# Hybrid decoder layer on one core: the mixer's output projection by seven block products for eight

## The reference, cut to what matters

```python
y = jax.nn.sigmoid(ga) * (att @ w_attn_br[l]) + jax.nn.sigmoid(gm) * (hm @ w_mlstm_br[l])
x = x + y @ w_out[l]          # (512 x 2048) @ (2048 x 2048): the product that is changed

hc = rms_norm(x, norm_cross[l])
cq = (hc @ w_cq[l]).reshape(b_, s_, CROSS_HEADS, CROSS_HEAD_DIM)
```

## Time and profile before

| what | before |
|---|---|
| median of 3 runs | 2763.83 us (2763.59 to 2771.11) |
| profiled execution | 2762.1 us, which is its span; nothing else is recorded of it |
| busy PE | 2716.5 us, 98% |
| busy DVE | 1951.8 us, 71% |
| busy ACT | 1205.3 us, 44% |
| granted TensorE clock | 0.995 of full speed in the mean |

### The profile page before, as it was taken

How to read it: one execution, slowest core, us unless ns; L and a number is a source line. 1 busy time by engine, 2 the same in 40 slices (tenths; PEclk the granted TensorE clock), 3 DMA queues, 4 the chain that set the end, 5 groups by cost and what they waited for, 6 DMA issues and landing times.

```text
span 2762.1 us, 35868 instructions
## 1 busy us (share of the span) xinstructions
PE 2716.5 (98%) x13169; PEld 2276.6 (82%) x13169; DVE 1951.8 (71%) x2483; ACT 1205.3 (44%) x1603; POOL 130.2 (5%) x194
## 2 busy tenths in 40 slices
PE   8999999999999999999998999999999999999998
PEld 7888888888788888888877888888888888888886
DVE  6674345454576556642346999999998999999998
ACT  6342234343433223322336566666665433333334
POOL 1000000000000000000000011111110000000000
PEclk9999999999999999999999999999999999999999
DMA  7454233324253222552214677777779955556533
GB/s 276 174 192 139 91 105 106 106 91 147 104 190 98 101 99 92 172 187 92 90 61 119 195 214 216 244 235 236 210 233 320 384 198 193 213 213 225 201 115 114
DMA packets 192136, 469.07 MB, mean 170 GB/s; under 512 B 11706, under 2 KB 32299, under 8 KB 180267
## 3 DMA queue, kind: packets, MB, share of 16 engines
q1 hardware_dynamic: 141512, 374.44, 38.6%
q10 hardware_dynamic: 33122, 76.61, 7.3%
q0 software_dynamic: 17408, 16.78, 4.2%
HBM read 366.08 MB, written 84.93 MB: 163 GB/s over the span
## 4 chain that ended last, share of the span: by engine, by line
PE 94%; DVE 2%; DMA 1%; ACT 1%; issue 1%; POOL 0%; ACTq 0%; DVEq 0%; POOLq 0%
PE acc L2281 13%; PE acc L2283 13%; PE acc L2282 13%; PE acc L2735 8%; PE aux L2735 6%; PE acc L2736 4%; PE acc L2765 4%; PE acc L2767 4%; PE acc L2769 4%; PE aux L2765 3%; PE aux L2769 3%; PE aux L2767 3%; PE aux L2736 3%; PE acc L2389 1%; PE acc L2393 1%; PE aux L2393 1%
## 5 line engine op out<-in xcount | busy, mean ns | idle before, releaser
L909 ACT ACTIVATE fhi<-flat 128x1024 fp32r<-128x1024 f32 x400 | 422.8, 1059 | 483.2 <-PE aux L2769 139.4
L1456 DVE TENSOR_TENSOR flo<-flat,fhi 128x1024 fp32r<-128x1024 f32 x400 | 487.2, 1220 | 70.6 <-ACT fhi L909 65.0
L1451 DVE TENSOR_TENSOR wlo<-raw,whi 128x2048 fp32r<-128x2048 f32 x112 | 256.7, 2292 | 310.6 <-ACT whi L895 309.7
L2281 PE MATMUL acc<-act_hi,whi 128*128 128x512 f32 x1024 | 406.8, 397 | 2.1 <-DVE vaug L1583 1.4
L2283 PE MATMUL acc<-act_hi,wlo 128*128 128x512 f32 x1024 | 400.0, 391 | 0.0
L2282 PE MATMUL acc<-act_lo,whi 128*128 128x512 f32 x1024 | 399.1, 390 | 0.0
L895 ACT ACTIVATE whi<-raw 128x2048 fp32r<-128x2048 f32 x112 | 213.8, 1909 | 298.8 <-PE acc L2283 282.6
L2281 PEld LDWEIGHTS acc<-act_hi,whi 128*128 128x128 f32 x1024 | 192.4, 188 | 43.7 <-issue 2.8
L2283 PEld LDWEIGHTS acc<-act_hi,wlo 128*128 128x128 f32 x1024 | 192.2, 188 | 41.1
L2282 PEld LDWEIGHTS acc<-act_lo,whi 128*128 128x128 f32 x1024 | 192.6, 188 | 37.4
L2735 PE MATMUL acc<-t,fhi 128*128 128x512 f32 x512 | 184.9, 401 | 12.4 <-issue 5.1
(11 more groups left out here) (393 smaller groups left out, 5675.0 us busy)
## 6 DMA issues: line engine op xcount, KB each, us to landing
raw<-in_w_in SPq DMA_DIRECT2D x64, 1024.0 KB, 5.1
flat<-in_w_up SPq DMA_DIRECT2D x64, 1024.0 KB, 7.7
flat<-in_w_down SPq DMA_DIRECT2D x64, 1024.0 KB, 5.1
hid_scratch<-staged ACTq DMA_DIRECT2D x112, 512.0 KB, 6.8
side_P<-hid_scratch SPq DMA_DIRECT2D x56, 1024.0 KB, 7.3
flat<-in_w_in SPq DMA_DIRECT2D x16, 1024.0 KB, 5.5
raw<-in_w_out SPq DMA_DIRECT2D x16, 1024.0 KB, 5.1
flat<-flat POOLq DMA_DIRECT2D x64, 256.0 KB, 3.8
```

Of the source, the lines that this page charges most:

```text
L909: nc.scalar.activation(tiles(fhi[ring(b, n)][:], down), unit_source(b, down, n), ACT.Copy).then_inc(unit_hi, 1)
L1451: nc.vector.tensor_tensor(wlo[n % 2][:], raw[n % 4][:], whi[n % 2][:].bitcast(F32), ALU.subtract).then_inc(lo_ready, 1)
L1456: nc.vector.tensor_tensor(tiles(flo[ring(b, n)][:], down), unit_source(b, down, n), tiles(fhi[ring(b, n)][:], down).bitcast(F32), ALU.subt ...
L2281: nc.tensor.matmul(dst, s_hi, v_hi, start=first, stop=False)
```

## The change

The output projection is made of four wide blocks of 14 units: for each half of the 2048 output columns, one block for y's tiles 0 to 7 and one for 8 to 15. The four sums of y's quarters that the products P6, P7, P5 and P3 need are made while y is made: `y_sums(i)` takes the two tiles 2i and 2i+1, ACT rounds them (`y_sums_hi`), DVE takes the rest (`y_sums_lo`), and ACT's queue stores both parts in DRAM (`store_y_sums`), from which SP loads them into `y_place` for each block. There is one staging pair, so `y_sums_hi(i)` waits for the store of sum i-1. The landing is `out_land`: two instructions on 128x512 for each product.

```diff
-N_WIDE = 4
+N_WIDE = 8
...
+Y_PLACE = {"P6": 0, "P7": 1, "P5": 2, "P3": 3}
+Y_SUMS = ("P6", "P7", "P5", "P3")
+X_SUMS, N_SUMS = 8, 16
...
+    out_blocks = [Wide_no(4 + i, G_CQ // 4 + 4 + i + 1, i == 0, out=i // 2) for i in range(4)]
+    out_blocks[3].set = 2
...
-        wide_blocks(w_out_v, G_OUT, 0, 1, 4)
...
+        sp.wait_ge(granule_used, G_CQ)
+        sp.wait_ge(y_sum_stored, Y_STORES + 32 * 7)
+        for name in Y_SUMS:
+            load_y_sum(out_blocks[0], name)
+        sp.wait_ge(y_sum_stored, Y_STORES + 32 * 8)
+        for j in range(2, 4):
+            residual(j)
+        for b, following in zip(out_blocks, out_blocks[1:]):
+            load_y_sum(following, "P6", b.units(6))
+            load_y_sum(following, "P7", b.units(8))
+            load_out(0, following, unit_lo, b.units(9))
+            load_out(1, following, unit_lo, b.units(10))
+            load_y_sum(following, "P5", b.units(10))
+            load_out(2, following, unit_lo, b.units(13))
+            load_out(3, following, unit_lo, b.units(14))
+            load_y_sum(following, "P3", b.units(UNITS))
...
+        def y_sums_hi(i):
+
+            act.wait_ge(sum_ready, X_SUMS + i + 1)
+            if i:
+                act.wait_ge(y_sum_stored, Y_STORES + 32 * i)
+            nc.scalar.activation(y_stage[0][:], y_sum_f[i % 2][:], ACT.Copy).then_inc(side_hi, 1)
+
+        def store_y_sums(i):
+
+            act.wait_ge(side_lo, X_SUMS + i + 1)
+            for part in range(2):
+                act.dma_start(y_sums_dram[i // 4, :, :, part, i % 4, :].rearrange("s p n -> p s n"),
+                              y_stage[part][:].bitcast(F32)).then_inc(y_sum_stored, 16)
+
         for j in range(4):
             for g in range(2):
-                split(G_MBR + 2 * j + g + 1)
+                if 2 * j + g < 7:
+                    split(G_MBR + 2 * j + g + 1)
+                if g == 0 and j:
+                    y_sums_hi(2 * j - 1)
+                elif j:
+                    store_y_sums(2 * j - 1)
+            if j == 3:
+                act.wait_ge(granule_used, G_CQ - 1)
+                unit_split_hi(out_blocks[0], 0, True)
+                unit_split_hi(out_blocks[0], 1, True)
...
+                if k % 4 == 2:
+                    y_sums_hi(2 * j)
+            store_y_sums(2 * j)
...
+        for q, b in enumerate(out_blocks):
+            for n in range(0 if q else 2, UNITS):
+                unit_split_hi(b, n, True)
+                if (q, n) == (0, 4):
+                    y_sums_hi(7)
+                if (q, n) == (0, 6):
+                    store_y_sums(7)
+                if q == 2 and n >= 6:
+                    out_squares(n - 6)
+                if q == 3 and n >= 7:
+                    query_input_hi(n - 7)
...
+        def y_sums(i):
+
+            f, first, second = y_sum_f[i % 2], ysum[0], ysum[1]
+            upper, lower = slice(0, 256), slice(256, 512)
+            step(nc.vector.tensor_tensor(f[:, 1, :], first[:, upper], first[:, lower], ALU.subtract))
+            step(nc.vector.tensor_tensor(f[:, 0, :], second[:, lower], f[:, 1, :], ALU.subtract))
+            step(nc.vector.tensor_tensor(f[:, 2, :], f[:, 0, :], first[:, upper], ALU.add))
+            nc.vector.tensor_tensor(f[:, 3, :], second[:, upper], f[:, 0, :], ALU.subtract).then_inc(sum_ready, 1)
...
+                if m == 1:
+                    y_sums(2 * j)
+                elif m == 2:
+                    y_sums_lo(2 * j)
+                elif m == 3 and j < 3:
+                    y_sums(2 * j + 1)
...
+        for n in (2, 3):
+            unit_split_lo(out_blocks[0], n, True)
+        for n in range(4):
+            weight_sum(out_blocks[0], DOWN_MIX_POS[n], True)
+        y_sums(7)
+        for q, b in enumerate(out_blocks):
+            for n in range(0 if q else 4, UNITS):
+                if q and n in (1, 3):
+                    out_land(out_blocks[q - 1], {1: "P4", 3: "P3"}[n])
+                if n in (5, 7, 9, 11, 13):
+                    out_land(b, PRODUCTS[(n - 5) // 2])
+                unit_split_lo(b, n, True)
+                if n in DOWN_MIX_POS:
+                    weight_sum(b, DOWN_MIX_POS[n], True)
+                if (q, n) == (0, 5):
+                    y_sums_lo(7)
+                if q == 3 and n >= 7:
+                    query_input_lo(n - 7)
+        out_land(out_blocks[3], "P4")
+        split(G_CQ)
+        query_input_lo(7)
+        out_land(out_blocks[3], "P3")
...
+            for n in range(UNITS):
+                wide_unit(b, n, banks_out, {name: (Y_PLACE[name], Y_LOADS // 16 + q + 1) for name in Y_SUMS}, (y_place, lambda p: y_place_loaded[p]), y_quarter)
+                if q == 3 and n >= 6:
+                    x1_tile(n - 6)()
```

More of the change, by code:

```diff
@@ L103, with __init__ @@
 SUM_LOADS = ((5, 5), (3, 0))
+Y_PLACE = {"P6": 0, "P7": 1, "P5": 2, "P3": 3}
+Y_SUMS = ("P6", "P7", "P5", "P3")
+X_SUMS, N_SUMS = 8, 16
 class Wide_no:
-    def __init__(self, i, loads):
-        self.turn, self.first, self.rows, self.opens, self.loaded = 0, i, i % 2, i % 2 == 0, 16 * (loads + i % 2 + 1)
+    def __init__(self, i, loads, opens=True, out=None):
+        self.turn, self.first, self.rows, self.opens = 0, i, i % 2, opens
+        self.loaded = 16 * loads
+        self.out, self.set = out, 1 - i % 2 if out is None else i % 2
     def units(self, i):
@@ L509, in mix_of @@
     def mix_of(b, u):
-        return wide_mix[b.first // 2][u] if isinstance(b, Wide_no) else mix[u]
+        if not isinstance(b, Wide_no):
+            return mix[u]
+        return wide_mix[b.first // 2][u] if b.out is None else out_mix[u]
     def unit_source(b, down, n):
@@ L523, in x_quarter, with y_quarter @@
         return part[:, 8 * row + 4 * rows:8 * row + 4 * rows + 4, 256 * half:256 * (half + 1)]
+    def y_quarter(part, rows, row, half):
+        return part[:, 8 * rows + row:8 * rows + 8:2, 256 * half:256 * (half + 1)]
     def sums_at(rows, name):
@@ L1204, in _, with squares @@
                 nc.scalar.activation(act_hi[:, k, :], ysum[k % 2][:], ACT.Copy).then_inc(y_hi, 1)
-        def squares(blk, m, j, done, before, turn=0):
-            act.wait_ge(bank_free[m], freed(blk, m, turn))
+                if k % 4 == 2:
+                    y_sums_hi(2 * j)
+            store_y_sums(2 * j)
+        def squares(ready, count, m, j, done, before):
+            act.wait_ge(ready, count)
             if before is not None:
@@ L1230, in _ @@
             query_input_hi(k)
+        for i in range(12, 16):
+            out_squares(i)
         split(G_CQ + 2)
@@ L2571, in _ @@
                     hooks={} if j else {(0, 1): [unit_transposes(NG - 1)]})
-        with pe.Fori(0, 3) as i:
-            product(B_OUT, G_OUT, 4, tokens(act_hi, act_lo), turn=i, n_per=4, inputs=waits(y_hi, y_lo))
         def residual_transposes(k, blk, full, hi, lo):
```

153 lines of the change are left out of this document (98 added, 55 removed).

## The result

The changed kernel takes 2800.4 us in the median of four runs (2795.8 to 2803.2) against 2763.8, 37 us slower; the ratio on record, made of all runs and not of the two medians, is 1.0123, interval 1.0103 to 1.0142. Forecast were 2783 and a range up to 2797: the direction came, the loss is twice the predicted one.

What follows compares the result with a forecast made beforehand. PE, busy 98% of the span, was taken to bound the kernel. Waits of 9.3 + 16.2 + 9.0 + 3.3 = 37.8 us, less 21.8 removed, plus 3 for the clock, gave 2763.8 + 19 = 2783 us, range 2770 to 2797.

Steps and rivals of the forecast that it cites:

- the landing L: mLSTM output: time from a sum store's second issue until it lands, taken as 7.5 us between ends of 4.9 and 12.7.
- share evenly: mLSTM output: stores and simultaneous loads split the transfers equally, so a second MB passes first, adding 2.6 us to 4.9.
- the 3 that stood for the clock: After waits: 3 us lost to slower matmuls, at unit 4 of the first block and perhaps once in the last.
- Removed, 21.8 us: Output projection: 672 matmuls in place of 768, so 96 fewer at 0.2266 us each, saving 21.8 us.
- The mLSTM output, 9.3 us: Waits of 0.9 us in the first block, 4.2 each in second and third, from a chain period of L + 18.5.
- The start, 16.2 us: First projection block: PE waits 9.5 us at unit 2, 5.5 plus 0.6 at unit 4, some 0.3 at two landings.
- S: Start of the last mLSTM granule; PE's work through unit 1 was to last until S + 16.3, fourth tile at S + 20.7.
- The last block and the query product, 12.3 us: Last projection block: three 3.0 us waits at units 8, 10 and 12, 9.0 us; query product's first granule, 3.3 us.
- (c): Rival: stores land last (L = 12.7) or the clock falls at every wait; about 2796 us, chance 0.12.
- (b): Rival: stores land as if alone (L = 4.9) and the clock holds; +8 us, 2772, chance 0.18.
- (e): Rival: the last block's chain of waits is not there; 9 to 12 us less, 2771 to 2774, chance 0.05.
- (d): Rival: added DVE work fits its idle time in the mLSTM output and at the start; 2754 us, faster, chance 0.05.

Runs made afterwards that it cites:

- loads_behind: Changed kernel with SP holding each mLSTM block's two weight loads (and w_out's first two) until the store issued at that moment has landed: 2803.0 us, ratio 1.0124.
- best_two: Changed kernel with weight loads ahead, query edits, reordered DVE work, a second staging pair, and w_out's loads first at the first hand-over: 2760.6 us, ratio 0.9962.
- the two edits that name their cause: Changed kernel with query input one unit later, 2791.0 us; then also the query product's first granule split ahead of the last query tiles and squares, 2787.2 us.
- fillers: Changed kernel with useless matmuls put into PE's long waits to hold the clock, no wait for another engine removed: 2796.6 us, ratio 1.0106.
- after_again: The changed kernel, unchanged, profiled a second time: 2802.0 us.
- before_again: The kernel before the change, unchanged, profiled a second time: 2772.5 us.
- two_pairs: Changed kernel with a staging pair of their own for sums 1, 3 and 5, two residual loads moved behind: 2792.4 us, ratio 1.0080.
- ahead_two: Changed kernel with weight loads ahead of the gate tiles in SP's queue and a second staging pair for sums 1, 3 and 5: 2789.9 us, ratio 1.0084.
- inputs_later: Changed kernel with ACT and DVE making the query input one unit later in the last projection block: 2791.0 us, ratio 1.0065.

## Why the prediction was right in direction and short in size

The step that failed first is the landing L, and with it "share evenly"; a wait at the hand-over of blocks was missing altogether. PE reaches the up projection 30.9 us late where 19 were forecast. The 12 us between are 5.0 more in the mLSTM output, 3.1 at the start, 3.2 at the hand-over, 2.2 in the last block and at the query product and 2.8 behind it, less the 3 that stood for the clock and 1.1 of an earlier start.

**Removed, 21.8 us.** Right: 96 matmuls, and the others kept 0.2267 us wherever nothing slowed them.

**The mLSTM output, 9.3 us.** L = 7.5 was too small. It was 9.5, 9.7 and 11.3 us, the chain's period 27.9 and 28.1 in place of 26.0, 4.0 us more for two blocks. The rest of the walk held (period minus L is 18.4 for the 18.5 of the prediction). loads_behind shows that the loads beside it make the difference (5.5 to 5.7 us with the gate tile alone, 4.1 with nothing). The prediction took 4.9 us and added 2.6 for the sharing, while the measured 9.5 is 5.4 above the store alone: the store did not get half of the bytes but 38% of the bytes, and 20% among w_out's rows of 4 KB, where L was largest although 1 MB less was issued. That packets and not bytes share evenly is read from the trace; no run changed the length of the rows. Three of the six waits, 3.1 us, are for DVE's evacuations (`ysum`), which the prediction did not list. What I had not seen is a second chain of the same length: the weights that leave SP's queue at that moment and are split right behind the sum. With the stops it came to 14.3 us of waits and rest.

**The start, 16.2 us.** 9.92 at unit 2 for 9.5, 3.71 at unit 4 for 6.1, then none where I had small ones; with 5.7 of rest 19.3 us, close to 16.2 and its clock. The match at unit 2 is chance: with S = 1198.16 the fourth tile came at S + 24.4 for S + 20.7, by an L of 11.3, but PE's own work also lasted until S + 19.4 for S + 16.3, since its matmuls were slow. At unit 4 the landing alone counted, as the sum's load took 4.9 us for the 7.1 and was there 5 us earlier.

**The hand-over to the second block, nothing.** A step that was missing: w_out's loads land in 10.5 us in the median, behind the residual and the sums in SP's queue, and cost 2.4 us in three waits, 3.2 with the rest. In best_two, where w_out stands first, none of the three is left.

**The last block and the query product, 12.3 us.** Right: 8.5 for 9.0 and 3.19 for 3.3, removed by the two edits that name their cause.

**Waits against time.** That 37.8 us of waits were forecast and found is chance: too little in the mLSTM output and at the hand-over, too much at unit 4, and slow matmuls that stood in for waits. The sum lacked the 0.27 us of each of 15 stops, 4 us. The 3 us for the clock were right in the sense of the text (slow matmuls behind which PE waits again cost nothing; fillers shows it) and too few behind the last wait: 2.8 us are lost from the query product on in this profile, none in after_again. Up to the up projection: 29.25 - 1.14 (an earlier start) + 2.80 = 30.9 us, 1532.31 against 1501.40.

**Beyond it.** The up projection took 645.2 us for 637.6, 7.5 more at the same granted clock, in this profile. No part of the change: the same pace stands in before_again. Up to the up projection the change costs 30.9 us in the first pair of profiles and 31.5 in the second (1531.76 against 1500.26), 12 more than forecast; the lowest times, 2795.8 and 2763.6, are 32 apart, but their pace was not profiled. The medians add some 5 by chance.

**The rivals.** (c), 2796, came nearest: its L of 12.7 was nearly reached in the last block (11.3); its other half, a clock that falls at every wait, was not (0.47 us matmuls behind 2.81). (b) fell with L, (e) with the three waits of 2.8 us. (d) asked for a landing in under 3.2 us; even the store alone takes 4.1. The rule of the Trainium skill ("DMA: Bandwidth & Descriptors", section "Anatomy of one DMA"), an estimate of 4.4 us for the store, agrees with the store alone (4.5 us from its first issue, 4.1 from its second) and is 5 below the store among loads; the measurement decides. With 4.4 for L the sum would have been some 10 us smaller (three times 3.1, and the 0.6), not 8.

## What to carry to other kernels

When a transfer is put on a chain, list what else starts at that moment on every queue, and what is waited for behind each of them: taking away one of two landings of like length gained half of the mLSTM output's loss (two_pairs) or nothing (loads_behind), both together nearly all (ahead_two). Between two queues count packets, not only bytes: here a store in rows of 1 KB got a fifth of the bytes beside loads in rows of 4 KB. Loads whose slots are free should not stand in an in-order queue behind one that waits for the computation. A wait that sits behind another engine's chain can't be cured by keeping PE's clock up: cut the chain (inputs_later, 10 us for two moved calls).

## What was not expected of the hardware

- PE at a granted clock of 1.00 has two paces in the up projection, 0.347 and 0.353 us for a 512- and a 256-column matmul, 10 us in 640. They go with the execution; in nine of the 14 profiles the pace changes once, between 1640 and 1680 us, in either direction, in best_two twice. The down projection shows none of it (389 ns in all). Why is open.
- A wait of 2.8 us is followed by slow matmuls or not: 0.47 us at 1372.59 and 1392.89, 0.76 at 1382.08. The Trainium skill ("TensorE: Matmul & The Clock Gate", section "The HAM clock gate") has idle time take the array to 1.2 GHz; the row at 1382.08 agrees (starts 0.43 us apart behind it), its two neighbours show no fall.
- A store of 1 MB lands 4.1 us behind its second issue with nothing beside it, and in 5.5 to 5.7 with one load of 256 KB. In the first two mLSTM blocks, with 1 to 3 MB of loads issued within 6 us on the other queue, it takes 8.3 to 10.2 us in the profiles; in the third, beside two granules of w_out in rows of 4 KB, 11.2 to 11.6 in all six profiles that have it so.
